# The recurrent layer's decay constants, formed between units of the first down projection

## What is computed

```python
def conv_ffn(x, w_up, conv_w, conv_b, w_down):       # both layers of the first block
    u = causal_dwconv(x @ w_up, conv_w, conv_b)
    g, v = u[..., :D_FF], u[..., D_FF:]
    return (jax.nn.gelu(g, approximate=True) * v) @ w_down

def rglru_mixer(...):                                # mixer of the second layer
    ...
    r = jax.nn.sigmoid(jnp.einsum('bsnc,ncd->bsnd', xr, ga_w) + ga_b)
    log_a = LRU_C * r * jax.nn.log_sigmoid(lam)      # lam: 1024 numbers
    a = jnp.exp(log_a)
```

## Time and profile before

| | us |
|---|---|
| median of 3 runs | 1409.62 |
| lowest and highest | 1407.47, 1410.17 |
| span of the profiled execution | 1409.4 |
| PE busy | 1325.8 (94%) |
| DVE busy | 924.0 (66%) |
| ACT busy | 689.8 (49%) |

### The profile page before, as it was taken

How to read it: one execution, slowest core, us unless ns; L and a number is a source line. 1 busy time by engine, 2 the same in 40 slices (tenths; PEclk the granted TensorE clock), 3 DMA queues, 4 the chain that set the end, 5 groups by cost and what they waited for, 6 DMA issues and landing times.

```text
span 1409.4 us, 19347 instructions
## 1 busy us (share of the span) xinstructions
PE 1325.8 (94%) x7808; PEld 1136.6 (81%) x7808; DVE 924.0 (66%) x1461; ACT 689.8 (49%) x1108; POOL 79.0 (6%) x129
## 2 busy tenths in 40 slices
PE   7999999898999999989999999999888989899997
PEld 4899988776788887977888876778778987688886
DVE  4444543347888857677888877565987655766665
ACT  4444444345666655566666755343421114455553
POOL 1000000001000001001000001022122100000000
PEclk9999999999999999999999999999999999999999
DMA  9644334536555557337555545313430003655451
GB/s 363 248 151 163 120 120 148 210 128 246 179 179 179 186 200 284 122 126 285 186 194 195 195 169 210 110 70 120 148 127 1 1 1 120 227 191 180 179 196 73
DMA packets 31813, 230.16 MB, mean 163 GB/s; under 512 B 11200, under 2 KB 14656, under 8 KB 18800
## 3 DMA queue, kind: packets, MB, share of 16 engines
q1 hardware_dynamic: 25712, 217.75, 43.1%
q10 hardware_dynamic: 5008, 7.54, 1.4%
q0 software_dynamic: 1008, 3.67, 0.7%
HBM read 225.50 MB, written 3.44 MB: 162 GB/s over the span
## 4 chain that ended last, share of the span: by engine, by line
PE 80%; DVE 11%; ACT 5%; issue 2%; POOL 1%; DMA 0%; DVEq 0%; POOLq 0%; ACTq 0%
PE ps L425 18%; PE ps L597 15%; PE ps L197 11%; PE ps L476 10%; PE ps L429 9%; PE ps L467 5%; PE ps L564 5%; PE ps L536 3%; DVE parts L333 3%; PE ps L508 2%; ACT parts L329 2%; DVE arena L1512 1%; DVE arena L279 1%; DVE arena L1848 1%; DVE hall L282 1%
## 5 line engine op out<-in xcount | busy, mean ns | idle before, releaser
L333 DVE TENSOR_TENSOR parts<-ring,parts 128x1024 fp32r<-128x1024 f32 x354 | 432.4, 1225 | 286.4 <-ACT parts L329 217.2
L329 ACT ACTIVATE parts<-ring 128x1024 fp32r<-128x1024 f32 x354 | 373.2, 1057 | 303.9 <-PE ps L429 104.8
L425 PE MATMUL ps<-hall,parts 128*128 128x512 f32 x1120 | 399.4, 401 | 8.5 <-DVE parts L333 4.2
L429 PE MATMUL ps<-hall,parts 128*128 128x256 f32 x1120 | 316.1, 282 | 0.0
L597 PE MATMUL ps<-parts 128*128 128x512 f32 x1128 | 264.9, 394 | 12.0 <-DVE parts L364 9.8
L425 PEld LDWEIGHTS ps<-hall,parts 128*128 128x128 f32 x1120 | 212.1, 189 | 63.5 <-issue 5.6
L597 PEld LDWEIGHTS ps<-parts 128*128 128x128 f32 x1128 | 211.8, 189 | 62.6 <-DVE parts L364 15.6
L429 PEld LDWEIGHTS ps<-hall,parts 128*128 128x128 f32 x1120 | 213.8, 191 | 0.0
L197 PE MATMUL ps<-arena 128*128 128x128 f32 (+2 forms) x1238 | 168.4, 297 | 22.6 <-DMA arena<-in_rel_bias 6.9
L197 PEld LDWEIGHTS ps<-arena 128*128 128x128 f32 (+1 forms) x1238 | 157.0, 198 | 31.7 <-issue 13.1
L476 PE MATMUL ps<-hall,parts 128*128 128x256 f32 x1152 | 140.4, 284 | 0.7 <-ACT arena L1079 0.7
(11 more groups left out here) (214 smaller groups left out, 1071.2 us busy)
## 6 DMA issues: line engine op xcount, KB each, us to landing
ring<-in_W SPq DMA_DIRECT2D x100, 2048.0 KB, 8.1
arena<-distance_tables SPq DMA_DIRECT2D x8, 384.0 KB, 7.5
gains<-in_gains POOLq DMA_DIRECT2D x5, 512.0 KB, 7.4
ring<-in_W SPq DMA_DIRECT2D x4, 512.0 KB, 9.1
arena<-in_gate_w ACTq DMA_DIRECT2D x1, 2048.0 KB, 10.4
matrices<-arena ACTq DMA_DIRECT2D x8, 256.0 KB, 2.8
x<-in_x SPq DMA_DIRECT2D x1, 1024.0 KB, 5.8
gates<-in_ada_gate_b POOLq DMA_DIRECT2D x2, 512.0 KB, 6.4
```

What stands on the lines that cost most here:

```text
L329: return nc.scalar.activation(unit_weights(n, 0, weights), weights, ACT.Copy)
L333: return nc.vector.tensor_tensor(unit_weights(n, 1, weights), weights, unit_weights(n, 0, weights), ALU.subtract)
L425: last = nc.tensor.matmul(ps[:, b, :].rearrange("p (a b) -> p a b", a=2), w[:, 0, :], hparts[:, :, k, :], start=k == 0, stop=False)
L429: last = nc.tensor.matmul(ps[:, b, 0:S], w[:, 1, :], hparts[:, 0, k, :], start=False, stop=k == KT - 1)
```

## The change

The call of `gated_ffn` for the first layer moves ahead of the decay constants on both engines. The constants are then formed between units of the first down projection. DVE does the three instructions up to the minimum after unit 7, the first eleven of the series after unit 9, the other seven after unit 11, and the last four after unit 13. ACT does its Exp after unit 9. `log1p_exp_neg` gets a function that it calls in the middle of the series. The other caller of it passes none.

```diff
--- before.py
+++ after.py
@@ -1131,9 +1131,10 @@
             n_ffn0.evacuate(act, 0)
             high_parts(act, up_ffn0.upto(0))
             act.dma_start(lgw[:, :, :, :, :], A["gate_w"]).then_inc(S_("gate_w_in"), 16)
+            gated_ffn(0, up_ffn0)
+            high_parts(act, p_ffn0.first + 10)
             act.wait_ge(S_("lam_abs"), 1)
             nc_a.activation(tmpc[:, 0:8], tmpc[:, 0:8], ACT.Exp).then_inc(S_("lam_exp"), 1)
-            gated_ffn(0, up_ffn0)
             p_ffn0.scalar(act)
             r_ffn0.square(act, 0)
             r_ffn0.square(act, 1)
@@ -1518,7 +1519,7 @@
                     v.tensor_tensor(aT[:, 2 * j:2 * j + 2, :], gl[j % 2][:, :, :], u[j % 2][:, 2:4, :], ALU.mult).then_inc(S_("aT"), 1)
                     low_parts(dve, up.upto(j + 1))
 
-            def log1p_exp_neg(e, w, w2, acc, n):
+            def log1p_exp_neg(e, w, w2, acc, halfway=None):
 
                 link(v.tensor_scalar(w, e, 2.0, None, ALU.add))
                 link(v.reciprocal(w, w))
@@ -1526,6 +1527,8 @@
                 link(v.tensor_tensor(w2, w, w, ALU.mult))
                 link(v.tensor_scalar(acc, w2, 2.0 / 15, 2.0 / 13, ALU.mult, ALU.add))
                 for c in (11, 9, 7, 5, 3, 1):
+                    if c == 5 and halfway:
+                        halfway()
                     link(v.tensor_tensor(acc, acc, w2, ALU.mult))
                     link(v.tensor_scalar(acc, acc, 2.0 / c, None, ALU.add))
                 link(v.tensor_tensor(acc, acc, w, ALU.mult))
@@ -1544,18 +1547,21 @@
             low_parts(dve, up_ffn0.first + NPARTS)
             low_parts(dve, up_ffn0.upto(0))
 
+            gated_ffn(0, up_ffn0)
+            low_parts(dve, p_ffn0.first + 8)
             dve.wait_ge(S_("par_in"), 16)
             v.tensor_scalar(small[:, 112:128], pcol("ga_b", 0, 16), 0.5, None, ALU.mult)
             lam = pcol("lam", 0, 8)
             link(v.tensor_scalar(tmpc[:, 0:8], lam, -1.0, None, ALU.mult))
             v.tensor_tensor(tmpc[:, 0:8], tmpc[:, 0:8], lam, ALU.min).then_inc(S_("lam_abs"), 1)
+            low_parts(dve, p_ffn0.first + 10)
             dve.wait_ge(S_("lam_exp"), 1)
-            log1p_exp_neg(tmpc[:, 0:8], tmpc[:, 8:16], tmpc[:, 16:24], tmpc[:, 24:32], 8)
+            log1p_exp_neg(tmpc[:, 0:8], tmpc[:, 8:16], tmpc[:, 16:24], tmpc[:, 24:32], lambda: low_parts(dve, p_ffn0.first + 12))
+            low_parts(dve, p_ffn0.first + 14)
             link(v.tensor_scalar(tmpc[:, 0:8], lam, 0.0, None, ALU.min))
             link(v.tensor_tensor(tmpc[:, 0:8], tmpc[:, 0:8], tmpc[:, 24:32], ALU.subtract))
             v.tensor_scalar(small[:, 128:136], tmpc[:, 0:8], 4.0, None, ALU.mult)
             v.tensor_scalar(small[:, 136:144], tmpc[:, 0:8], -4.0, None, ALU.mult).then_inc(S_("lru_consts"), 1)
-            gated_ffn(0, up_ffn0)
             p_ffn0.vector(dve)
             r_ffn0.gained(dve, 0)
             r_ffn0.add(dve, 0)
@@ -1733,7 +1739,7 @@
                 link(v.tensor_scalar(z1, z0, -1.0, None, ALU.mult))
                 v.tensor_tensor(z1, z1, z0, ALU.min).then_inc(S_("sp_in"), 1)
                 dve.wait_ge(S_("sp_exp"), 1)
-                log1p_exp_neg(z1, z2, z3, z4, 40)
+                log1p_exp_neg(z1, z2, z3, z4)
                 link(v.tensor_scalar(z0, z0, 0.0, None, ALU.max))
                 link(v.tensor_tensor(z0, z0, z4, ALU.add))
                 link(v.tensor_scalar(z0, z0, -1.0, None, ALU.mult))
```

## The result

The changed kernel takes 1402.99 us (median of 20 runs) and the kernel before 1408.28 us (median of 20 runs). The ratio is 0.9962, with a 95% interval from 0.9950 to 0.9975: faster by 5.3 us, and by 3.5 to 7.0 with the interval. The forecast was 5.7 us less. Timed once more in another set of runs it was 1402.91 against 1408.32 us, ratio 0.9969 (0.9951 to 0.9986), which is 4.4 us less, 2.0 to 6.9 with the interval.

What follows compares the result with a forecast made beforehand. PE, busy 94% of the 1409.4 us span, was taken to bound the kernel. Up projection 5.72 us back, down projection 0 and gates 0 made 5.7 us off: 1403.9 us, range 1401.5 to 1407.0.

Steps and rivals of the forecast that it cites:

- 3.72 us of waits: First up projection: PE's waits for DVE's low parts, 1.16 us ahead of unit 7 and 2.56 ahead of unit 8, go.
- 1.80 of slow clock: First up projection: unit 8 took 4.63 us instead of 2.83; the 1.80 us of slow clock go.
- 0.22 of refilling: First up projection: unit 7 took 0.22 us more than 2.83, refilling a pipeline that stood empty; this goes.
- the comparison with the second layer: Up projections, unit 3 done to unit 8 done: 14.13 us in the second layer, 19.85 in the first, 5.72 us difference.
- the rival in which a slow stretch comes back elsewhere: Behind 350 us: the waits go but a slow stretch appears elsewhere, leaving 3.9 us saved, 1405.7 us; chance 0.17.
- The reserve ahead of unit 8: First up projection: unit 8's low part would be ready 0.9 us before PE needs it, as in the second layer.
- The gelu's table load: First up projection, ACT behind unit 8's split: a 1.28 us load put at nothing, at most 0.4 us if not covered.
- The down projection: First down projection: the moved instructions fit the room, unit 10 keeping 1.4 us of reserve; cost 0 us, upper bound 6.5.
- The table load: ACT behind unit 9 of the down projection: 1.30 us is the whole switch; its removal at the gates gives 0 us.
- The stall in the down projection: Down projection: PE waits for low parts of units 10 to 14, time 1410 to 1412 us; chance 0.05.
- the second wait went with the first: Up projection, against the rival that only the first wait goes, saving 1.4 us, 1408.2 us; chance 0.08.
- a fall of the clock at new places: Anywhere in the kernel: the clock falling where it did not before would show the prediction wrong; no size given.

Runs made afterwards that it cites:

- full chain: Kernel before, in three traces, and kernel before with one unread Exp added on ACT behind unit 9 (ratio 1.0004): all the constants' steps stay ahead of the up projection.
- half ahead: Kernel before with seven series steps and the last four instructions moved into the down projection, the Exp and eleven steps staying ahead: 1405.79 us, ratio 0.9980.
- waits filled: Kernel before with 4 and 10 extra matmuls on PE ahead of its waits for units 7 and 8: 1405.32 us, ratio 0.9995.
- Exp ahead: Kernel before with all 18 series steps and the last four instructions moved into the down projection, the minimum and Exp staying ahead: 1400.21 us, ratio 0.9960.
- one piece: Changed kernel with the 18 series steps and four last instructions in a single stretch behind unit 9: 1403.74 us, ratio 0.9969 to before.
- left out: Changed kernel without the minimum, the Exp and the 18 series steps, the constants being simple multiples of lam: 1403.05 us, ratio 0.9958 to before.
- changed again: The changed kernel, unaltered, timed and traced once more beside the kernel before: 1402.91 us, ratio 0.9969.
- series done twice: Kernel before with the 18 series steps repeated on DVE ahead of the first sum: 1410.76 us, ratio 1.0034.

## Why the prediction was right

*The size.* The sum was 3.72 us of waits, 1.80 of slow clock and 0.22 of refilling. The distance fell from 19.85 to 14.13 us, 5.72 us, as the comparison with the second layer had said. The measured time fell by 5.3 us, with 3.5 to 7.0 for the interval. The time alone could not tell this from the 3.9 us of the rival in which a slow stretch comes back elsewhere. The traces can: the slow clock is there in all four traces of the full chain and in none of the changed kernel's two. One term was mis-sized inside the sum. The 1.80 us were called slow clock, but unit 8 takes 3.09, 3.12 and 3.11 us behind a wait at full clock (half ahead, waits filled, Exp ahead). So 0.26 to 0.29 us of them are the slower start, and the slow clock costs about 1.5 us. The sum stays the same. That is why filling the waits gave back 1.6 us and not 2.

*What is late next.* The reserve ahead of unit 8 was given as 0.9 us, from the second layer. It is 0.9 us in the changed kernel (352.47 against 353.37), and the run with half of the chain ahead gives 0.8. The gelu's table load cost nothing: it ends at 350.17, and ACT then waits 1.19 us for DVE before the gelu.

*The down projection.* The step said 0.1 us late on ACT, 1.1 us late for unit 10's low part, a reserve of 1.4 us, and 0.2 to 0.3 us for unit 12. Measured: 0.1, 1.1 (491.26 against 487.46 + 2.72), 1.5 and 0.2. The run in one piece used up the reserve and made the wait of 0.66 us that follows from it. The run without the series puts the price at nothing (219.42 against 219.39 us).

*The table load.* The forecast took 1.30 us for it from the earlier trace rows and called that the whole. The Trainium skill, "ScalarE: Activation LUTs", section "What ACT_TABLE_LOAD costs", states a drain of 1.38 us on top of 1.28, 2.66 us in all. Here ACT's input split begins at 487.03, the load at 487.45, and the Exp at 488.74. Elsewhere in the same trace an instruction follows an input split 0.30 us after its start (477.57 to 477.87), so the load costs 1.4 us in all, 0.1 of it ahead of the load. The 1.30 us of the forecast were 0.1 too small. An estimate by the page's 2.66 us would put the Exp near 490.1. The measurement decides, for this place.

*The rivals.* The stall in the down projection did not happen, and the second wait went with the first. Slow stretches did move elsewhere: between the first two traces those near 610 and 940 us differ in length, and other traces have them near 230, 547, 858, 998 or 1136 us as well. The forecast had called a fall of the clock at new places a sign of being wrong; the changed kernel's second trace has falls near 854, 994 and 1130 us that its first trace lacks, so they move in executions of one and the same kernel. Traces of before have the first and the last too (859 and 1135 us). The middle one is in four of the six traces of kernels whose first sum comes earlier than in before (left out, one piece, half ahead, changed again), and in none of the six others. Whether the change makes it likelier stays open.

*What I had not seen.* The cover of 1.24 us that I took for the experiments, from 4.96 - 3.72, was wrong by 0.4 us, and the sum for the series done twice (23.5 us, measured 21.95) by 1.6 us. In both, a slow PE overlaps with a wait that follows it. Waits, slow clock and refilling add up only if nothing behind them waits again.

## What to carry to other kernels

Work on a few columns that no step needs soon is not free for being small: 25 instructions of 0.2 us each in front of the first sum cost 5.7 us, since every engine works in order and the sum stood behind them. If the same order of work runs a second time without them, its trace gives both the gain and the next reserve. The same steps cost nothing where what stands behind them is ready early enough. Pieces of 2.3 and 1.4 us are longer than DVE's idle of 1.1 us between units, and yet PE does not wait, since the low parts had been ready early. A reserve worked out from the rows (need less ready) tells how large a piece may be: 1.5 us were left behind the piece of 2.3, and the piece of 4.3 us made a wait of 0.66.

## What the runs showed of the hardware

**PE has two speeds at one granted clock.** The third up projection in both kernels, window by window (columns as above):

```profile
core 0: us, PE busy (x) PEld busy (x) DVE busy (x) ACT busy (x) POOL busy (x), PEclk, DMA share, GB/s
1240.00:1340.00 100.00, 100.00 (x579) 88.19 (x578) 66.17 (x65) 51.74 (x56) 0.00 (x0) 1.00 0.53 190
```

```profile
1235.00:1335.00 100.00, 100.00 (x568) 86.74 (x567) 65.16 (x64) 51.31 (x56) 0.00 (x0) 1.00 0.52 186
```

Both have the clock at 1.00 and PE busy all the time, but 579 matmuls in one and 568 in the other. A chunk takes 11.09 us in one and 11.31 in the other, 2% apart. Ten chunks give the 2.2 us by which the changed kernel fell back in the first pair of traces. In twelve traces with three up projections each only these two values appear in a steady stretch. The short one is in the third up projection in five traces (before, one piece, half ahead, Exp ahead, the changed kernel's second), in most of the first and in the second in both further traces of before, and in the first with the series twice. It is not fixed by the kernel: before has it in the third in one trace and in the first two in others.

The speed can change inside a projection, at a place where PE stands still. The rows of ACT in the section on half of the chain ahead show it. Units 1 to 3, ahead of the wait of 2.19 us, take 8.32 us (330.71 to 339.03). Units 9 to 11, behind it, take 8.48 (355.37 to 363.85), and the clock is 1.00 all along. In the second trace of before it goes the other way: 8.48 us ahead of the waits (333.78 to 342.26) and 8.32 behind them (361.90 to 370.22). What sets the speed stays open, and nothing here was tried on it. With the slow stretches it is a part of why one kernel's runs spread over 8 us (1404.68 to 1412.36 for before), while the two waits of its up projection are the same within 0.05 us in its three traces.

**A wait may or may not be followed by the half clock.** At 2.5 us of PE standing still it came four times of four, twice before PE resumed and twice 0.9 us after. It also came inside the wait of 4.85 us. Behind 2.19 us it did not, in one trace. That run has no first wait ahead of it either, so these traces give no length of wait at which the clock falls. With the waits filled by 14 matmuls whose results are overwritten the clock stayed up, in one trace.
